# Splitting weights as soon as their slot is free, in the mixing and output stages of a two-block transformer kernel

## The reference, cut to what matters

```
h  = rmsnorm(x, g_mix)
z  = h @ w_in                                # pool part, q, k, v
y_pool = pool_mixer(u_pool, w_pool_grp) * pool_scale     # 4 groups, windows 2, 4, 8, 16
y_attn = diff_attention(q, k, v, ...)        # two softmaxes per head, their difference, head norm
gates  = sigmoid(h @ w_gate + b_gate)
merged = gates[:, :D] * (y_pool @ w_branch_pool) + gates[:, D:] * (y_attn @ w_branch_attn)
x = x + merged @ w_out
x = x + square(relu(rmsnorm(x, g_ffn) @ w_up)) @ w_down
```

## Time and profile before

| | us |
|---|---|
| median of 3 runs | 3246.98 (3244.05 to 3247.95) |
| the profiled execution, its own time | 3247.09 |
| its span, first to last instruction | 3245.3 |
| TensorE (PE) busy | 2880.6 |
| VectorE busy | 1254.8 |
| ScalarE busy | 1133.7 |
| POOL busy | 719.8 |

### The profile page before, as it was taken

One profiled execution on the slowest core, in us unless ns is written; L12 is line 12 of the kernel. 1 busy time (PEld: TensorE's weight loads), 2 busy tenths in 40 slices (PEclk: granted clock), 3 DMA queues, 4 the chain that ended last, 5 costly groups with the idle time before them and its releaser, 6 DMA issues.

```text
span 3245.3 us, 38040 instructions
## 1 busy us (share of the span) xinstructions
PE 2880.6 (89%) x13672; PEld 2303.4 (71%) x13672; DVE 1254.8 (39%) x1751; ACT 1133.7 (35%) x1585; POOL 719.8 (22%) x387
## 2 busy tenths in 40 slices
PE   5999998987787875878997998988699899999999
PEld 3888886876666664657786666666478688888887
DVE  5544423135555554353001555655532421212121
ACT  3212223234555454232213566666411321212120
POOL 0222221213334332112222111111022122222222
PEclk8999999999999997889999999999799999999999
DMA  4333312441211111201232100001141111111112
GB/s 191 130 119 126 116 58 88 166 147 46 85 46 46 51 45 39 85 26 63 89 127 80 33 33 33 26 33 52 42 175 48 39 46 52 45 52 45 52 45 97
DMA packets 62569, 236.80 MB, mean 73 GB/s; under 512 B 6944, under 2 KB 7584, under 8 KB 59936
## 3 DMA queue, kind: packets, MB, share of 16 engines
q1 hardware_dynamic: 62496, 235.88, 20.8%
HBM read 191.81 MB, written 44.04 MB: 73 GB/s over the span
## 4 chain that ended last, share of the span: by engine, by line
issue 51%; PE 35%; POOL 5%; DVE 4%; ACT 3%; DMA 1%; POOLq 0%; ACTq 0%; DVEq 0%; SPq 0%
PE PS L542 26%; POOL WL L1800 5%; PE PS L748 3%; PE PS L722 2%; PE PS L700 2%; DVE bC L1553 1%; PE PS L685 1%; ACT PS L1096 1%; DVE ATL L1375 1%; ACT bB L1095 1%; POOL dBIAS L1855 1%; ACT ATH L1088 0%; DMA TMP<-mods 0%; PE PS L705 0%; DVE bQL L1375 0%
## 5 line engine op out<-in xcount | busy, mean ns | idle before, releaser
L1800 POOL TENSOR_TENSOR WL<-WR,WH 128x1024 fp32r<-128x1024 f32 x215 | 520.8, 2422 | 2137.3 <-ACT WH L978 2131.3
L542 PE MATMUL PS<-HH,WH 128*128 128x512 f32 x2272 | 728.5, 402 | 122.5 <-issue 36.8
L542 PE MATMUL PS<-HL,WH 128*128 128x512 f32 x2272 | 714.0, 396 | 0.0
L542 PE MATMUL PS<-HH,WL 128*128 128x512 f32 x2272 | 712.1, 395 | 0.0
L542 PEld LDWEIGHTS PS<-HH,WH 128*128 128x128 f32 x2272 | 427.4, 192 | 228.8 <-issue 95.0
L542 PEld LDWEIGHTS PS<-HL,WH 128*128 128x128 f32 x2272 | 435.8, 192 | 93.7
L542 PEld LDWEIGHTS PS<-HH,WL 128*128 128x128 f32 x2272 | 434.9, 191 | 93.3
L978 ACT ACTIVATE WH<-WR 128x1024 fp32r<-128x1024 f32 x214 | 225.5, 1054 | 543.0 <-PE PS L542 366.0
L542 PE MATMUL PS<-GH,WH 128*128 128x512 f32 x768 | 236.7, 389 | 1.6 <-DVE TMP L1770 1.5
L542 PE MATMUL PS<-GH,WL 128*128 128x512 f32 x768 | 236.4, 389 | 0.0
L542 PE MATMUL PS<-GL,WH 128*128 128x512 f32 x768 | 236.4, 389 | 0.0
(11 more groups left out here) (226 smaller groups left out, 3482.5 us busy)
## 6 DMA issues: line engine op xcount, KB each, us to landing
WR<-wst SPq DMA_DIRECT2D x215, 512.0 KB, 3.5
TMP<-mods SPq DMA_DIRECT2D x48, 512.0 KB, 3.7
MRAW<-mods SPq DMA_DIRECT2D x16, 512.0 KB, 10.1
v_hl<-VS SPq DMA_DIRECT2D x8, 1024.0 KB, 6.4
bV<-v_hl SPq DMA_DIRECT2D x8, 1024.0 KB, 7.8
X<-xt SPq DMA_DIRECT2D x4, 1024.0 KB, 7.9
x_b<-X SPq DMA_DIRECT2D x8, 512.0 KB, 4.9
k_hi<-KSH SPq DMA_DIRECT2D x8, 512.0 KB, 4.9
```

Source lines behind the costliest of these rows:

```text
L542: last = pe.matmul(PS[:, dst0 + q:dst0 + q + HALF], l, rr[:, k * S + q:k * S + q + HALF], start=a, stop=z)
L1800: pool.tensor_tensor(WL[slot][:, :], WR0[:, :], WH[slot][:, :].bitcast(F32), ALU.subtract).then_inc(w_lo, 1)
```

## The change

In the pool, gate and output chunks ScalarE's split is tied to the end of the chunk that frees the slot, and stands ahead of the work on that chunk's result. It is now one chunk further ahead in the program (c + 2 instead of c + 1). The split for C_GP behind the gate loop is thereby inside the loop. In the output stage the first weight load is issued ahead of the loads of g_a and m_p, and the others stand one round earlier. TensorE's wait for dBD moves from ahead of the first QKV chunk to behind it.

```diff
@@ SP, output stage
             for k in range(KT):
                 sp.dma_start(kt(X, k), x_d[k]).then_inc(ld_xr, 16)
+            load_w(C_AB + 2)
             sp.wait_ge(f_lo, FILL["ab"] + KT)
             for n in range(KT):
                 if n >= 2:
                     sp.wait_ge(g_lo, KT + n - 1)
                 sp.dma_start(T[n % 2], g_a[n]).then_inc(ab_ld[n % 2], 16)
                 sp.dma_start(T[2 + n % 2], m_p[n]).then_inc(ab_ld[n % 2], 16)
-                load_w(C_AB + 2 + n)
+                if n < KT - 1:
+                    load_w(C_AB + 3 + n)
@@ TensorE, first QKV chunks
-            pe.wait_ge(d_st, 16)
             for n in range(3):
                 chunk(C_QKV2 + n, (C_QKV2 + n) % 2, 0, ud[0] + n)
+                if n == 0:
+                    pe.wait_ge(d_st, 16)
                 if n < 2:
                     group_sums(n + 1)
@@ ScalarE, mixing stage
             for g in range(4):
                 c = C_POOL + g
-                if g:
-                    split_w(c + 1, (c + 1) % 2)
                 act.wait_ge(chunk_done, c + 2)
+                split_w(c + 2, c % 2)
                 act.activation(TP, PAIR[c % 2], ACT.Identity).then_inc(free[c % 2], 1)
...
             with act.Fori(0, KT // 2) as i:
                 for m in range(2):
                     s = (C_GA + m) % 2
-                    split_w(2 * i + (C_GA + m + 1), 1 - s)
                     act.wait_ge(chunk_done, 2 * i + (C_GA + m + 2))
+                    split_w(2 * i + (C_GA + m + 2), s)
                     act.activation(T[2], PAIR[s], ACT.Sigmoid, bias=vec("b_gate", 2 * i + (8 + m))).then_inc(free[s], 1)
                     act.wait_ge(ga_st, 32 * i + 16 * (m + 1))
-            split_w(C_GRP + 1, (C_GRP + 1) % 2)
@@ ScalarE, output stage
+            split_w(C_AB + 1, (C_AB + 1) % 2)
             for n in range(KT):
                 c = C_AB + n
-                split_w(c + 1, (c + 1) % 2)
+                if n < KT - 1:
+                    act.wait_ge(chunk_done, c + 2)
+                    split_w(c + 2, c % 2)
                 act.wait_ge(ab_m, n + 1)
                 act.activation(kt(GH, n), T[2 + n % 2], ACT.Identity).then_inc(g_hi, 1)
```

## The result

| | before | after |
|---|---|---|
| median of the runs, us | 3247.95 (5 runs, 3244.05 to 3253.67) | 3214.8 (5 runs, 3211.55 to 3218.4) |
| span of the profiled execution, us | 3245.3 | 3211.7 |
| mean granted clock of TensorE | 0.954 | 0.959 |

The ratio is 0.9898, with a 95% interval of 0.9885 to 0.9911: 33 us less, 29 to 37. The forecast was 3216, the range 3211 to 3223.

A forecast was written before the change was run, and what follows sets the result against it. TensorE, busy for 89% of the span, was taken as the bound, so only its stops and low clock could be won back. 16.2 + 10.7 + 4.0 = 30.9 us saved gave 3216 us, range 3211 to 3223.

The forecast's parts named there:

- Part 1: Mixing stage: earlier weight splits remove TensorE's 11.3 us of waits for WL and the low clock behind them; 16.2 us saved.
- the first rival: Mixing stage: POOL pays for overlapping VectorE, its first split ends 1.4 us late and TensorE waits; 29.5 saved, chance 0.12.
- Part 2: Start of the second QKV stage: moving the wait for dBD removes most of that stop and its low clock; 10.7 us saved.
- The two terms of the sum: First QKV chunk: 8.4 us from a shorter stop ahead of it, 2.3 from no low clock in it.
- The step that failed: Behind the first QKV chunk: ScalarE's split, behind dRS and lambda, ends at 1745.0, so its copy starts on time, costing nothing.
- Part 3: Output stage of the second attention: earlier weight load and split let TensorE start the third chunk sooner; 4.0 us saved.
- I charge 2.0: Output stage: TensorE's remaining 2.7 us stop lowers its clock, costing 2.0 us against 1.6 before.
- the third rival: Output stage: the stop is short enough to keep the clock; 6.0 us saved instead of 4.0, 3214.2 us, chance 0.08.
- The second: Rival, output stage: the weight lands no earlier than before; 1.8 us saved instead of 4.0, 3218.4 us, chance 0.10.
- the fourth: Rival, first QKV chunk: the clock falls there all the same; 8.7 us saved instead of 10.7, 3218.2 us, chance 0.07.
- the fifth: Rival, later stages: one starts sooner but is paced by something not moved; no change, 3247 us, chance 0.03.
- the sixth: Rival, gate chunks: ScalarE's row of split, sigmoid and store becomes the bound; slower, say 3255 us, chance 0.02.

The follow-up runs named there:

- e4: Kernel before with the new split order in the four pool rounds only, the gate loop splitting as before; 3238.89 us, ratio 0.9987.
- e9: Kernel after with X's eight loads issued one per output round instead of ahead of the output stage's first transfers; 3216.09 us, ratio 0.9905.
- e10: Kernel after with the second QKV chunk's split ahead of the lambda wait, X's loads spread over rounds, dRS and dBD loaded before dBIAS; 3215.04 us, ratio 0.9907.
- e2: Kernel before with only TensorE's wait for dBD moved behind the first QKV chunk; 3234.86 us, ratio 0.9969.
- e8: Kernel after with ScalarE's split for the second QKV chunk moved ahead of its wait for the lambda chain; 3214.78 us, ratio 0.9905 to before.
- e3: Kernel before with only the output stage changed, on the SP queue and on ScalarE; 3241.77 us, ratio 0.9983.
- e5: Kernel before with the new split order in the gate chunks only, the pool rounds splitting as before; 3243.55 us, ratio 0.9996.
- e6: Kernel before with the output stage's new load order on the SP queue only, ScalarE's order old; 3269.32 us, ratio 1.0074.
- e1: Kernel before with only the mixing stage changed, pool and gate chunks; 3230.43 us, ratio 0.9948.

## Why the prediction was right, and where its terms were off

The sum was 30.9 us, and the three stretches gave 30.7. The terms, one by one:

**Part 1, forecast 16.2, measured 16.5.** Right in mechanism and in size. No wait for WL, ten chunks in 108.9 us (forecast 108.8), the group products' later sigmoid hidden as forecast: a stop of 1.0 for it, and 3.8 for YPL where e4, with the old order there, has 4.8. The price of the overlap was mis-sized: VectorE lost 2.1 us, not 1.4, and POOL 0.3 (2.76 against 2.43), where I had let only one of them pay. It cost nothing in the profiled execution, but only just: POOL's first end lay 0.1 us before it was wanted (forecast 0.4), and the 0.7 us left for chunk 3's weight were used up (POOL ended at 1467.48, the chunk was wanted at 1456.6 + 10.88 = 1467.5). In e9's and e10's POOL took longer, and TensorE waited 0.7 to 0.8. So the first rival was no other case than the forecast; it happens in some executions and costs about half of its 1.4. The Trainium skill, GPSIMD Engine Reference, Specifications, has the two engines contend when VectorE reads two inputs from SBUF; the trace agrees, with 9.65 against 11.79 us on one side and 2.43 against 2.52 to 3.50 on the other.

**Part 2, forecast 10.7, measured 8.1 in the kernel after, 9.7 alone (e2).** The two terms of the sum held: the stop ahead of the first QKV chunk fell from 9.9 to 1.3 us and the chunk from 13.2 to 11.0, together 10.8. What was lost came behind them. The step that failed is "ScalarE's split for the next chunk stands behind dRS and the lambda chain, 1743.94 to 1745.0, so its copy of the chunk starts on time". I had carried dRS's landing over unchanged from before. It landed after 4.8 us instead of 3.5 in three of the four executions that had TensorE at work there and the loads in this order, and ScalarE's copy began 1.0 us late: the stop ahead of the group sums is 2.98 to 3.12 us in these three (after, e2, e9), and 2.18 in e8 and e10, where dRS landed after 3.5 and 2.0. The rest, 1.6 us, is the clock, which fell at the group sums. I had taken it to stay up there, from one row of before; the next group sums of the same trace, behind the same stop of 2.03, ran at the lower clock (3.66 us). In the kernel after the second group sums kept the clock (1.98 us), so this part of the loss comes back one chunk later: by the start of the third QKV chunk the change has given 9.8 us, and 11.4 in e2.

**Part 3, forecast 4.0, measured 6.1, 4.5 alone (e3).** Right in mechanism: the third output chunk's start is set by VectorE's multiplication behind m_p. From the first matmul of the stage to this start it is 2335.14 - 2318.43 = 16.7 us, forecast 2364.3 - 2347.3 = 17.0; in e3 and e8 it is 16.7 too. Mis-sized in the kernel after were the stop and, with it, the term "I charge 2.0": the stop was 1.41 us, not 2.7, mostly because TensorE reached it 1.0 us later: the first stretch took 15.30 at a clock of 0.80, in before 14.31 at 0.86. Behind it nothing was paid for the clock. That is the third rival, to which I gave 0.08. In e3 and e8 the first stretch took 14.4 and 14.3, the stop was 2.27 and 2.40, the clock fell behind it as forecast, and the gain was 4.5 in both. So the forecast's case came in two of three executions, the third rival's in one. The weight landed 10.6 us after its issue, forecast 9.5, which a stop ended by m_p hides.

**Rivals.** The second (the weight lands late) did not come, nor did the fourth (low clock in the first QKV chunk), though a price close to its 2.0 us fell one step later; the fifth (given back later) and the sixth (ScalarE's row) are refuted by the ratio and by e5. That the errors of Parts 2 and 3 cancel, -2.6 against +2.1, is luck: both hang on the clock. My range allowed for both. By the later cut the three stretches gave 32.4 us, 1.5 more than the sum.

**Open.** Why dRS lands after 3.5 or 4.8 us with the same loads ahead of it. That the split behind dRS is what delays the copy rests on the order of the code and on the times in the rows; no run shows it by itself. That loads ahead of dRS matter is shown by e10 only together with the other two edits. Why the clock falls behind one short stop and not behind another of the same length (2.03 us, twice in before) is open as well.

## What to carry to other kernels

A step that prepares an operand belongs right behind the event that frees its slot, through the whole chain of stages; done for half of it, the delay comes due at the first place with the old order (e4), and a load moved up a queue without the step that lets it go holds all behind it (e6, +21 us). Where a stall is taken away, look at each engine that the next stage needs, not only at the one that stood still: here ScalarE waited for a small constant behind a large one. Where a clock has fallen somewhere in a row of like steps, cut the stretch behind the last of them: a fall that only moves looks like a loss in one stretch and a gain in the next. Whether the clock held is read from the whole chunk, not from its first pair. And a gain of one or two us at a single stop is not worth chasing while the clock behind the neighbouring stops moves by as much.

## What the runs showed of the hardware

- The same four group-sum matmuls took 1.98 and 3.66 us behind two stops of 2.03 in one execution (before), 1.96 behind a stop of 2.98 (e2), but 3.68 behind 2.03 (e1), 3.58 behind 2.03 (e8), 3.51 behind 3.02 (after), 2.85 behind 2.18 (e10). The length of the last stop alone does not tell whether the clock falls from 2.4 to 1.2 GHz.
- Behind the stops of 2.25 to 2.40 us inside rows of chunks (before, e3, e8) the first matmul pair still took 0.70 us, and the first pair of 1.00 or more came 1.0 to 1.5 us later.
- VectorE and POOL work on SBUF side by side at a price that can fall on either: 2.1 us on the multiplications of X and 0.1 to 1.1 on POOL's split beside them. In the output stage of the kernel after, VectorE's add of m_p, which now falls beside POOL's split in every steady round, took 3.43 us, where it takes 1.26 in a round in which it starts as that split ends. POOL's split took 2.39 there and lost nothing:

```profile
2349.79 1.26 DVE L1776 TENSOR_TENSOR TMP<-TMP,TMP 128x1024 f32<-128x1024 f32 x1
2358.48 3.43 DVE L1776 TENSOR_TENSOR TMP<-TMP,TMP 128x1024 f32<-128x1024 f32 x1
```

- A small constant queued behind a larger one landed 3.4 to 4.8 us after its issue, and 2.0 when it was issued first (e10).
